# A decoder step on one Trainium2 core: the dense part of the expert lookup narrowed from 384 to 368 tokens, the gathered part widened from 136 to 152

## The chip, the cores and the metric

The kernel is one program on one core of a Trainium2 chip. The metric is its device time in microseconds (us). Three runs of the kernel before took 1760.16, 1762.86 and 1763.15 us, so the median is 1762.86 us. One further execution was profiled and is the source of every row below.

## The reference: what is computed

One decoder layer for 512 prompt tokens and 8 single-token samples (520 tokens, width 1024). A mixer stage (retention and a short convolution) comes first. Then comes the expert lookup, which is the part that matters here:

```
q = xb @ w_q                               # per token: 8 heads x 2 halves x 128
s = q . keys                               # 8 x 2 x 128 scores
s1, i1 = top_k(s[:, :, 0], 16);  s2, i2 = top_k(s[:, :, 1], 16)
cand = s1[..., :, None] + s2[..., None, :]             # 16 x 16 per head
top_s, top_pos = top_k(cand, 16)                       # 16 experts per head
eidx = i1*128 + i2 (at top_pos);  gate = softmax(top_s)    # 128 experts per token, out of 16384
a    = gelu(einsum('pd,ped->pe', xb, u_tab[eidx]))
out  = einsum('pe,ped->pd', gate * a, v_tab[eidx])
```

The result goes through an RMS norm and is added to the residual.

## The kernel before

Every engine has its own program, written out by hand. The queues run in order and meet at semaphores. There is no scheduler.

**First expert stage (up to 1204 us).** For every key row `m` of 128 (128 experts each) TensorE computes the product of all 520 tokens with `u_tab` (L1711: each weight is split in a high and a low part, 3 products x 8 x 2 halves of 260 columns = 48 matmuls). ScalarE applies gelu (L1783), and SyncE stores the 128 x 520 result in DRAM (`ahead_dram`, `keep`). Beside it VectorE picks the experts, tile of tokens by tile of tokens (`select`, `decide`). The tiles are given by `EDGES`. For the first `SCATTERED` = 3 tiles (`ND` = 384 tokens) GpSimd scatters the gates into a dense array in DRAM (`gates_dram`, L99, 384 indirect DMAs with one gate per token each). This array was cleared by 24 DMAs and is laid out in chunks of `CH` = 32 tokens.

**Second expert stage (1204 to 1742 us).** The 128 steps `n` of this stage run over the key rows again, now with `v_tab`. Two ways of summing exist side by side:

- *Dense tokens (the first ND).* SyncE loads the stored products (`aa`, drawn from the buffer `qp`) and the gates (`gt`) for 4 steps at a time (L1615, L1617, two buffers each) and `v_tab` in pairs of 1024 KB (L1595, four buffers). VectorE multiplies products by gates (`coefficients`, L1934). ScalarE rounds to the high part `ch` (L1805) and the weights to `uh` (L1769). VectorE subtracts for the low parts `ul` (`low`, L1905) and `cl` (`low_coefficients`, L1939). TensorE does 3 x 8 = 24 matmuls of ND columns per step (L1734). Only the first 8 matmuls with `cl` at step 0 have 512 columns, to set all columns of the accumulators.
- *Gathered tokens (the other TG = 520 - ND = 136).* The 128 choices of each token are packed so that row `r` of `TG` rows holds one expert for each of 128 partitions. `GROUPS` lists them as (first token, tokens): the 8 samples, then 64 and 64 prompt tokens. With n tokens in a group, each token takes 128/n partitions and the group has n rows. For each row GpSimd issues one indirect DMA for the product (`ag`, L1863, 128 x 4 bytes, issued 8 rows ahead) and one for the expert's `v_tab` row (`vg`, L1870, 128 x 4 KB = 512 KB, four buffers, drawn from `qp`). VectorE adds it, scaled, to the group's sum `fg` (L1955) and first scales `ag` once in 8 rows (L1949). `summed(n)` spreads the rows evenly over the steps n = 8 to 123. After a group's last row TensorE adds its partitions up into the columns of its tokens (`gathered_sums`, L1695, 8 matmuls), at step 72 for the first group of 64 and at step 126 for the second. The group of samples is folded by DMAs and VectorE instead (L1962).

Within one step VectorE's order is: coefficients of step n+2, `ul` of step n, `cl` of step n+1, then the gathered rows that are due. GpSimd may not issue `vg` of row r before VectorE has summed row r-4.

**End (1742 to 1762 us).** Squares, norm and residual over 512 columns. This part does not depend on ND.

Of the kernel before, what the change touches and what calls it, by code (L numbers as in the profile page):

```python
# [9 lines left out]
ALU = mybir.AluOpType  # L10
# [3 lines left out]
P = 128  # L14
# [19 lines left out]
EDGES = (0, 128, 256, 384, 512, T)  # L34
# [4 lines left out]
GROUPS = ((128, 8), (0, 64), (64, 64))  # L39
CH = TT // 4  # L40
# [56 lines left out]
def scatter(nc, io, i, r):  # L97

    nc.gpsimd.indirect_dma_start(  # L99
        out=io["gates"].rearrange("g p c a t -> (g p c a t)").unsqueeze(1),  # L100
        out_offset=bass.IndirectOffsetOnAxis(ap=io["where"][:, i, r:r + 1], axis=0),
        in_=io["gate"][:, i, r:r + 1], in_offset=None, compute_op=ALU.add).then_inc(io["scattered"][i], 16)
# [250 lines left out]
def mixer_stage(nc, sem, sb, pair, halves, residual, on_chip, hh, hl, qp, io, w_dram):  # L353
# [3 lines left out]
    with stack:  # L357
# [178 lines left out]
        def sync_program(sp):  # L536
# [20 lines left out]
            for n in range(NSLOT, len(order)):  # L557
# [4 lines left out]
                if 0 <= c < CLEARS:  # L562
                    size = NGRP * 2 * SCATTERED // CLEARS
                    i, g = divmod(c * size, NGRP)
                    wide = TT // CH // 2
                    sp.dma_start(io["gates"][g:g + size, :, i * wide:(i + 1) * wide]
                                 .rearrange("g p c a t -> p g (c a t)"),
                                 blank[:].unsqueeze(1).to_broadcast([P, size, TT * GB // 2]))\
                        .then_inc(io["cleared"][i // 2], 16)
# [890 lines left out]
def peer_stage(nc, sem, sb, pair, halves, residual, on_chip, hh, hl, packed, qp, io):  # L1460
# [17 lines left out]
    TURN_AT = 72  # L1478
# [18 lines left out]
    with stack:  # L1497
# [26 lines left out]
        fg = sb(stack, "fg", [P, len(GROUPS), D])  # L1524
        folded = keys[:].rearrange("p j n -> p (j n)")[0:P // 2, 0:D]
        packed_choice = sb(stack, "packed_choice", [P, 3, TG])
        chosen = sb(stack, "chosen", [P, GROUPS[1][1]])
        ag = sb(stack, "ag", [P, TG])
# [4 lines left out]
        sample_rows, sample_squares = fg[0:NS, 0, :], folded[0:NS]  # L1533
# [47 lines left out]
        def sync_program(sp):  # L1581
# [54 lines left out]
            def fold(n):  # L1636

                if n:
                    sp.wait_ge(fold_ok, n)
                else:  # L1640
                    sp.wait_ge(fg_ok, GROUP_AT[1])
                w = FOLDS[n]
                sp.dma_start(folded[0:w], fg[w:2 * w, 0, :]).then_inc(fold_in, 16)
# [32 lines left out]
        def tensor_program(pe):  # L1676
# [12 lines left out]
            def gathered_sums(g):  # L1689

                first, n = GROUPS[g]
                pe.wait_ge(fg_ok, GROUP_AT[g + 1])
                pe.wait_ge(chosen_ok, 1)
                for k in range(KD):
                    nc.tensor.matmul(ps[:, k, ND + first:ND + first + n], fg[:, g, k * P:(k + 1) * P],  # L1695
                                     chosen[:], start=False, stop=False)
# [28 lines left out]
            for n in range(NK):  # L1725
# [14 lines left out]
                if n == TURN_AT:  # L1740
                    gathered_sums(1)
                if n == NK - 2:
                    gathered_sums(2)
# [136 lines left out]
        def vector_program(dve):  # L1880
# [61 lines left out]
            def gathered():  # L1942
# [11 lines left out]
                sums_of = fg[:, group_of(r), :]  # L1954
                nc.vector.scalar_tensor_tensor(sums_of, vg[:, r % NG, :], ag[:, r:r + 1], sums_of,  # L1955
                                               ALU.mult, ALU.add).then_inc(fg_ok, 1)

            def fold(n):

                w = FOLDS[n]  # L1960
                dve.wait_ge(fold_in, 16 * (n + 1))
                nc.vector.tensor_tensor(fg[0:w, 0, :], fg[0:w, 0, :], folded[0:w], ALU.add).then_inc(fold_ok, 1)  # L1962
# [23 lines left out]
            for m in range(lows[0], LAST):  # L1986
# [3 lines left out]
                if n == 0:  # L1990
                    coefficients(0)
                    coefficients(1)
                    nc.vector.tensor_scalar(cl[:, 0, ND:SEQ], ident[:, 0:SEQ - ND], 0.0, None, ALU.mult)
                    low_coefficients(0)
                if 0 < n <= len(GROUPS):
                    nc.vector.memset(fg[:, n - 1], 0.0)
                if n == len(GROUPS) + 1:
                    nc.vector.tensor_reduce(chosen[:], ident.rearrange("p (h t) -> p t h", t=GROUPS[1][1]), AX.X,
                                            ALU.add).then_inc(chosen_ok, 1)
# [138 lines left out]
```

## Time and profile before

| | |
|---|---|
| median of three runs | 1762.86 us (1760.16 to 1763.15) |
| the profiled execution | 1764.12 us, its span 1762.3 us |
| mean granted TensorE clock | 0.993 of full speed |
| PE busy | 1729.2 us, 98% of the span |
| DVE, POOL, ACT busy | 62%, 59%, 33% |
| memory traffic | 385.18 MB by DMA, mean 219 GB/s |

PE is TensorE's matmuls, PEld its weight loads, DVE VectorE, ACT ScalarE, POOL GpSimd and SP SyncE. The span runs from the first to the last instruction. Matmuls are pipelined: a single one takes longer from start to end than the distance to the next. So their pace is read from a stretch's length divided by the number of matmuls in it, and not from the mean of one. "share" of DMA is the mean busy share of the core's 16 DMA engines. It can come out slightly above 1, since packets of one engine may overlap.

### The profile page before, as it was taken

How to read it: one execution, taken by the hardware profiler on the slowest of the kernel's cores; microseconds unless marked ns; L12 is line 12 of the kernel's file. 1: busy time of each engine (PE TensorE's matmuls, PEld its weight loads, DVE VectorE, ACT ScalarE, POOL GpSimd, SP SyncE). 2: the span in 40 equal slices, each digit the busy share in tenths (PEclk: the TensorE clock that was granted, in tenths of full speed). 3: DMA queues.
4: the chain of work that ended last, by engine and by line, in shares of the span. 5: the costliest groups of instructions: out<-in, count | busy, mean ns of one | idle time of the engine just before them, and what ended most of it. 6: DMA issues, size and time to landing. Idle time of an engine off the chain costs nothing.

```text
span 1762.3 us, 31194 instructions
## 1 busy us (share of the span) xinstructions
PE 1729.2 (98%) x12708; PEld 1688.9 (96%) x12708; DVE 1097.6 (62%) x2208; ACT 587.3 (33%) x764; POOL 1043.2 (59%) x693
## 2 busy tenths in 40 slices
PE   7999999999999999999999999999999999999996
PEld 5999979699999999999999999999999999999996
DVE  6724686568577366667552221224888989888884
ACT  5222264333323333232232222223333333333332
POOL 0340100006777888888888888874677777767721
PEclk9999999999999999999999999999999999999997
DMA  8523399673566665766667666668999999999971
GB/s 328 195 97 144 99 374 311 224 233 82 109 128 145 127 145 110 151 127 140 143 132 153 138 134 145 133 139 332 360 368 377 378 346 369 368 368 372 377 293 49
DMA packets 192358, 385.18 MB, mean 219 GB/s; under 512 B 74376, under 2 KB 132104, under 8 KB 177368
## 3 DMA queue, kind: packets, MB, share of 16 engines
q1 hardware_dynamic: 111864, 306.56, 51.3%
q0 software_dynamic: 80352, 76.65, 20.2%
q8 instruction: 100, 1.64, 0.4%
q14 instruction: 42, 0.34, 0.1%
HBM read 318.44 MB, written 64.19 MB: 217 GB/s over the span
## 4 chain that ended last, share of the span: by engine, by line
PE 94%; DVE 5%; ACT 1%; issue 0%; DMA 0%; SPq 0%; DVEq 0%; ACTq 0%
PE ps L1711 42%; PE ps L1734 30%; PE ps L669 12%; PE ps L720 3%; PE ps L783 2%; PE ps L615 1%; PE ps L1685 1%; DVE wl L1153 1%; DVE rs L1182 1%; PE ps L807 1%; DVE tg L1372 0%; PE ps L750 0%; DVE first_low L1153 0%; PE ps L736 0%; DVE qp L2022 0%
## 5 line engine op out<-in xcount | busy, mean ns | idle before, releaser
L99 POOL DMA_INDIRECT gates_dram<-gate,where x384 | 643.0, 1675 | 266.3 <-issue 252.2
L1711 PE MATMUL ps<-hh,ul 128*128 128x260 f32 x2048 | 412.8, 283 | 0.0
L1711 PE MATMUL ps<-hl,uh 128*128 128x260 f32 x2048 | 412.8, 283 | 0.0
L1711 PE MATMUL ps<-hh,uh 128*128 128x260 f32 x2048 | 412.1, 283 | 0.0
L1905 DVE TENSOR_TENSOR ul<-us,uh 128x1024 fp32r<-128x1024 f32 x132 | 161.2, 1222 | 350.9 <-issue 291.3
L1734 PE MATMUL ps<-cl,uh 128*128 128x384 f32 (+1 forms) x1024 | 345.0, 337 | 1.6 <-issue 1.1
L1734 PE MATMUL ps<-ch,uh 128*128 128x384 f32 x1024 | 344.1, 336 | 0.0
L1734 PE MATMUL ps<-ch,ul 128*128 128x384 f32 x1024 | 344.1, 336 | 0.0
L1711 PEld LDWEIGHTS ps<-hl,uh 128*128 128x128 f32 x2048 | 315.7, 189 | 0.4 <-issue 0.4
L1711 PEld LDWEIGHTS ps<-hh,ul 128*128 128x128 f32 x2048 | 315.8, 188 | 0.0
L1711 PEld LDWEIGHTS ps<-hh,uh 128*128 128x128 f32 x2048 | 314.8, 188 | 0.0
L1783 ACT ACTIVATE a<-ps 128x520 f32<-128x520 f32 x128 | 77.5, 606 | 520.0 <-PE ps L1711 434.7
L1870 POOL DMA_INDIRECT qp<-vtab,packed_choice x136 | 184.2, 1355 | 102.7 <-DVE fg L1955 74.3
L1863 POOL DMA_INDIRECT ag<-ahead_dram,packed_choice x136 | 167.5, 1232 | 62.1 <-issue 41.2
L1734 PEld LDWEIGHTS ps<-cl,uh 128*128 128x128 f32 x1024 | 192.5, 188 | 2.3 <-issue 1.3
L1734 PEld LDWEIGHTS ps<-ch,ul 128*128 128x128 f32 x1024 | 192.5, 188 | 0.3
L1734 PEld LDWEIGHTS ps<-ch,uh 128*128 128x128 f32 x1024 | 192.5, 188 | 0.0
L1955 DVE SCALAR_TENSOR_TENSOR fg<-qp,ag,fg 128x1024 f32<-128x1024 f32 x136 | 174.1, 1280 | 11.7 <-DMA qp<-vtab,packed_choice 5.9
L1805 ACT ACTIVATE ch<-qp 128x384 fp32r<-128x384 f32 x128 | 67.2, 526 | 337.1 <-PE ps L1734 280.9
L1905 DVE TENSOR_TENSOR ul<-pairs,uh 128x1024 fp32r<-128x1024 f32 x124 | 150.9, 1217 | 0.8 <-ACT uh L1769 0.8
L1153 DVE TENSOR_TENSOR wl<-wr,wh 128x2048 fp32r<-128x2048 f32 x38 | 89.7, 2361 | 81.9 <-ACT wh L911 81.7
L1769 ACT ACTIVATE uh<-us 128x1024 fp32r<-128x1024 f32 x132 | 138.6, 1051 | 0.0
(248 smaller groups left out, 2238.8 us busy)
## 6 DMA issues: line engine op xcount, KB each, us to landing
us<-utab SPq DMA_DIRECT2D x128, 512.0 KB
pairs<-vtab SPq DMA_DIRECT2D x62, 1024.0 KB
gates_dram<-blank SPq DMA_DIRECT2D x24, 1024.0 KB, 10.1
ahead_dram<-a SPq DMA_DIRECT2D x128, 192.0 KB
qp<-ahead_dram SPq DMA_DIRECT2D x32, 768.0 KB
gt<-gates_dram SPq DMA_DIRECT2D x32, 768.0 KB
wr<-w_ada SPq DMA_DIRECT2D x21, 1024.0 KB, 7.9
wr<-w_in SPq DMA_DIRECT2D x13, 1024.0 KB, 4.7
```

The costliest lines, as they stand in the source:

```text
L99: nc.gpsimd.indirect_dma_start(out=io["gates"].rearrange("g p c a t -> (g p c a t)").unsqueeze(1), out_offset=bass.IndirectOffsetOnAxis(ap ...
L669: last = nc.tensor.matmul(pair(m % RING)[:, a, :], w, r[:, k, a * TH:(a + 1) * TH], start=(first and q == 0), stop=(final and q == 2))
L1153: nc.vector.tensor_tensor(low_buffers[b], raw_buffers[raw_slot(split[i])], high_buffers[b].bitcast(F32), ALU.subtract).then_inc(wl_ok, 1)
L1711: last = nc.tensor.matmul(out[:, half, :], w, r[:, k, half * TH:(half + 1) * TH], start=(k == 0 and q == 0), stop=(k == KD - 1 and q == 2))
L1734: last = nc.tensor.matmul(ps[:, k, columns], w, r[:, n % NL, columns], start=whole, stop=(n == NK - 1 and q == 2))
L1769: nc.scalar.activation(uh[:, m % NH], raw(m), ACT.Copy).then_inc(uh_ok, 1)
L1783: nc.scalar.activation(halves(a[:, m % NA]), pair(1 + m % 3), ACT.Gelu_apprx_tanh).then_inc(a_ok, 1)
L1805: nc.scalar.activation(ch[:, n % NL], aa[:, n // GB % NV, n % GB], ACT.Copy).then_inc(ch_ok, 1)
L1863: nc.gpsimd.indirect_dma_start(out=ag[:, at:at + 1], out_offset=None, in_=words, in_offset=bass.IndirectOffsetOnAxis(ap=packed_choice[:, 0 ...
L1870: nc.gpsimd.indirect_dma_start(out=vg[:, r % NG, :], out_offset=None, in_=values, in_offset=bass.IndirectOffsetOnAxis(ap=packed_choice[:, ...
L1905: nc.vector.tensor_tensor(ul[:, m % NH], raw(m), uh[:, m % NH].bitcast(F32), ALU.subtract)\
L1955: nc.vector.scalar_tensor_tensor(sums_of, vg[:, r % NG, :], ag[:, r:r + 1], sums_of, ALU.mult, ALU.add).then_inc(fg_ok, 1)
```

## The change

`EDGES` becomes (0, 128, 256, 368, 496, 520). The third scattered tile has 112 tokens, the two last tiles 128 and 24. ND becomes 368, and TG 152. A fourth group of 16 tokens (8 partitions per token, 16 rows) is summed behind the others. `CH` becomes 16, since 368 is no multiple of 32. The second turn on TensorE moves from step 126 to step 118, and a third one comes at step 126. The fourth sum lies on the `keys` buffer, which is free by then.

```diff
-EDGES = (0, 128, 256, 384, 512, T)
+EDGES = (0, 128, 256, 368, 496, T)
-GROUPS = ((128, 8), (0, 64), (64, 64))
-CH = TT // 4
+GROUPS = ((144, 8), (0, 64), (64, 64), (128, 16))
+CH = 16
@@ scatter
+    n = EDGES[i + 1] - EDGES[i]
-        out_offset=bass.IndirectOffsetOnAxis(ap=io["where"][:, i, r:r + 1], axis=0),
-        in_=io["gate"][:, i, r:r + 1], in_offset=None, compute_op=ALU.add).then_inc(io["scattered"][i], 16)
+        out_offset=bass.IndirectOffsetOnAxis(ap=io["where"][0:n, i, r:r + 1], axis=0),
+        in_=io["gate"][0:n, i, r:r + 1], in_offset=None, compute_op=ALU.add).then_inc(io["scattered"][i], 16)
@@ peer_stage
-    TURN_AT = 72
+    TURNS_AT = (72, 118, NK - 2)
-        fg = sb(stack, "fg", [P, len(GROUPS), D])
+        fg = sb(stack, "fg", [P, len(GROUPS) - 1, D])
+        on_keys = keys[:].rearrange("p j n -> p (j n)")
+        chosen_last = sb(stack, "chosen_last", [P, GROUPS[3][1]])
+        sums_of = [fg[:, g, :] for g in range(len(GROUPS) - 1)] + [on_keys[:, D:2 * D]]
@@ gathered_sums
-                pe.wait_ge(chosen_ok, 1)
+                pe.wait_ge(chosen_ok, 2)
-                    nc.tensor.matmul(ps[:, k, ND + first:ND + first + n], fg[:, g, k * P:(k + 1) * P],
-                                     chosen[:], start=False, stop=False)
+                    nc.tensor.matmul(ps[:, k, ND + first:ND + first + n], sums_of[g][:, k * P:(k + 1) * P],
+                                     (chosen if n == GROUPS[1][1] else chosen_last)[:], start=False, stop=False)
@@ tensor_program, behind step n
-                if n == TURN_AT:
-                    gathered_sums(1)
-                if n == NK - 2:
-                    gathered_sums(2)
+                if n in TURNS_AT:
+                    gathered_sums(1 + TURNS_AT.index(n))
@@ vector_program, behind step n
                 if 0 < n <= len(GROUPS):
-                    nc.vector.memset(fg[:, n - 1], 0.0)
+                    nc.vector.memset(sums_of[n - 1], 0.0)
                 if n == len(GROUPS) + 1:
                     nc.vector.tensor_reduce(chosen[:], ident.rearrange("p (h t) -> p t h", t=GROUPS[1][1]), AX.X,
                                             ALU.add).then_inc(chosen_ok, 1)
+                    nc.vector.tensor_reduce(chosen_last[:], ident.rearrange("p (h t) -> p t h", t=GROUPS[3][1]), AX.X,
+                                            ALU.add).then_inc(chosen_ok, 1)
```

The rest of the diff adapts the 24 clearing DMAs to 23 chunks and the zeros of `cl` to 144 columns. Since `pack` loops over the groups, it issues 12 small DMAs and not 9. Since the loop over chunks in the mixer's last part runs to TT/CH, 4 more tiny VectorE operations compute `token`.

**VectorE, from the gathered row of step 10 to that of step 11** of the second expert stage (`fg` is the sum of gathered rows, `qp` the products, `ul` and `cl` the low parts). Before:

```order
L1955 SCALAR_TENSOR_TENSOR fg<-qp,ag,fg 128x1024
L1934 TENSOR_TENSOR qp<-qp,gt 128x384
L1905 TENSOR_TENSOR ul<-pairs,uh 128x1024
L1939 TENSOR_TENSOR cl<-qp,ch 128x384
L1955 SCALAR_TENSOR_TENSOR fg<-qp,ag,fg 128x1024
```

The same place now:

```order
L1958 SCALAR_TENSOR_TENSOR fg<-qp,ag,fg 128x1024
L1937 TENSOR_TENSOR qp<-qp,gt 128x368
L1908 TENSOR_TENSOR ul<-pairs,uh 128x1024
L1942 TENSOR_TENSOR cl<-qp,ch 128x368
L1958 SCALAR_TENSOR_TENSOR fg<-qp,ag,fg 128x1024 x2
```

The chain of a step is the same, with 368 instead of 384 elements in two of its operations. A step with two gathered rows comes at 8, 11, 14 and 17, where before it came at 8, 13 and 19: 152 rows instead of 136 stand in the same 116 steps.

**TensorE, at step 126.** `chosen` and `chosen_last` are the 0/1 matrices that add up a token's partitions. Before:

```order
L1734 MATMUL ps<-ch,uh 128x384
L1734 MATMUL ps<-ch,ul 128x384
L1695 MATMUL ps<-chosen,fg 128x64 x8
L1734 MATMUL ps<-cl,uh 128x384
L1734 MATMUL ps<-ch,uh 128x384
```

Now:

```order
L1739 MATMUL ps<-ch,uh 128x368
L1739 MATMUL ps<-ch,ul 128x368
L1700 MATMUL ps<-chosen_last,keys 128x16 x8
L1739 MATMUL ps<-cl,uh 128x368
L1739 MATMUL ps<-ch,uh 128x368
```

The 8 matmuls with 64 columns that stood here stand 8 steps earlier, at step 118, and 8 with 16 columns are new. On GpSimd the alternation of `ag` and `vg` is the same, and 16 pairs longer.

## Rows read from the trace of the kernel before

**Rows 1.** The page: PE's total; 40 slices of DMA share and GB/s.

```profile
PE 1729.2 (98%) x12708; PEld 1688.9 (96%) x12708; DVE 1097.6 (62%) x2208; ACT 587.3 (33%) x764; POOL 1043.2 (59%) x693
...
DMA  8523399673566665766667666668999999999971
GB/s 328 195 97 144 99 374 311 224 233 82 109 128 145 127 145 110 151 127 140 143 132 153 138 134 145 133 139 332 360 368 377 378 346 369 368 368 372 377 293 49
```

**Rows 2.** Chain that ended last: start, length in us, what, how many instructions.

```profile
811.15 392.32 PE ps L1711 x3264
...
1204.61 238.35 PE ps L1734 x1368
...
1511.57 224.69 PE ps L1734 x1296
1736.27 1.73 PE ps L1695 x16
```

**Rows 3.** Line L1734: duration min/median/max in ns, first and last start.

```profile
L1734 PE MATMUL ps<-ch,ul x1024: 332/336/339, 1205.1 to 1741.9; 128*128 128x384 f32 x171
```

**Rows 4.** Steady stretch on DVE: start, us, operation; "x2" is two merged.

```profile
1479.89 2.67 DVE L1955 SCALAR_TENSOR_TENSOR fg<-qp,ag,fg 128x1024 f32<-128x1024 f32 x2
1482.47 0.55 DVE L1934 TENSOR_TENSOR qp<-qp,gt 128x384 f32<-128x384 f32 x1
1482.94 1.22 DVE L1905 TENSOR_TENSOR ul<-pairs,uh 128x1024 fp32r<-128x1024 f32 x1
1484.08 0.55 DVE L1939 TENSOR_TENSOR cl<-qp,ch 128x384 fp32r<-128x384 f32 x1
1484.55 1.28 DVE L1955 SCALAR_TENSOR_TENSOR fg<-qp,ag,fg 128x1024 f32<-128x1024 f32 x1
1485.74 0.55 DVE L1934 TENSOR_TENSOR qp<-qp,gt 128x384 f32<-128x384 f32 x1
```

**Rows 5.** Windows: length, busy us of each engine, PEclk, DMA share, GB/s.

```profile
1240.00:1700.00 460.00, 459.57 (x2656) 459.00 (x2656) 401.87 (x486) 163.75 (x223) 327.83 (x253) 1.00 0.98 369
...
1205.00:1710.00 505.00, 504.57 (x2914) 503.72 (x2913) 434.72 (x530) 179.97 (x244) 351.73 (x272) 1.00 0.97 366
```

**Rows 6.** DMA queues from 1240 to 1700 us: MB and share of 16 engines.

```profile
q1 hardware_dynamic: 16020, 101.48, 57.1%
q0 software_dynamic: 22512, 67.71, 40.2%
```

**Rows 7.** Windows with the densest DMA: mixer's weight loads; within the second stage.

```profile
230.00:270.00 40.00, 39.32 (x269) 32.02 (x269) 34.81 (x31) 23.95 (x36) 0.55 (x1) 1.00 1.04 393
...
1302.00:1332.00 30.00, 30.00 (x175) 30.00 (x174) 25.84 (x32) 10.92 (x15) 20.31 (x17) 1.00 1.02 377
```

**Rows 8.** The page, costliest groups on POOL: count, busy, mean ns, idle before.

```profile
L1870 POOL DMA_INDIRECT qp<-vtab,packed_choice x136 | 184.2, 1355 | 102.7 <-DVE fg L1955 74.3
L1863 POOL DMA_INDIRECT ag<-ahead_dram,packed_choice x136 | 167.5, 1232 | 62.1 <-issue 41.2
```

**Rows 9.** POOL in order of time: first wait for DVE; the last gather.

```profile
1238.00 1.95 POOL L1870 DMA_INDIRECT qp<-vtab,packed_choice  x1 [5.61 <-DVE fg L1955]
1240.26 1.31 POOL L1863 DMA_INDIRECT ag<-ahead_dram,packed_choice  x1 [0.30 <-issue]
...
1702.00 1.01 POOL L1870 DMA_INDIRECT qp<-vtab,packed_choice  x1 [1.12 <-DVE fg L1955]
```

**Rows 10.** Waits on DVE from 1210 to 1740 us: total, times, longest.

```profile
DVE cl L1939 <- ACT ch L1805: 45.1, 57, 2.5
...
DVE fg L1955 <- DMA qp<-vtab,packed_choice: 5.9, 5, 2.4
```

**Rows 11.** Line L1955: first and last start of the 136 gathered sums.

```profile
L1955 DVE SCALAR_TENSOR_TENSOR fg<-qp,ag,fg x136: 1267/1279/1312, 1236.4 to 1716.6; 128x1024 f32<-128x1024 f32 x136
```

More of the change, by code:

```diff
@@ L565, in sync_program @@
                     wide = TT // CH // 2
-                    sp.dma_start(io["gates"][g:g + size, :, i * wide:(i + 1) * wide]
-                                 .rearrange("g p c a t -> p g (c a t)"),
-                                 blank[:].unsqueeze(1).to_broadcast([P, size, TT * GB // 2]))\
+                    last = min((i + 1) * wide, NCH)
+                    some = (last - i * wide) * GB * CH
+                    sp.dma_start(io["gates"][g:g + size, :, i * wide:last].rearrange("g p c a t -> p g (c a t)"),
+                                 blank[:, 0:some].unsqueeze(1).to_broadcast([P, size, some]))\
                         .then_inc(io["cleared"][i // 2], 16)
@@ L1523, in peer_stage @@
         cl = sb(stack, "cl", [P, NL, SEQ], F32R)
[L1524 to L1525 removed]
+        fg = sb(stack, "fg", [P, len(GROUPS) - 1, D])
+        on_keys = keys[:].rearrange("p j n -> p (j n)")
+        folded = on_keys[0:P // 2, 0:D]
         packed_choice = sb(stack, "packed_choice", [P, 3, TG])
         chosen = sb(stack, "chosen", [P, GROUPS[1][1]])
+        chosen_last = sb(stack, "chosen_last", [P, GROUPS[3][1]])
         ag = sb(stack, "ag", [P, TG])
@@ L1532, in peer_stage @@
         squares = qp[:, 0:KD, :]
-        sample_rows, sample_squares = fg[0:NS, 0, :], folded[0:NS]
+        sums_of = [fg[:, g, :] for g in range(len(GROUPS) - 1)] + [on_keys[:, D:2 * D]]
+        sample_rows, sample_squares = sums_of[0][0:NS], folded[0:NS]
         ON_POOL = (0, 2, 4)
@@ L1642, in fold @@
                 w = FOLDS[n]
-                sp.dma_start(folded[0:w], fg[w:2 * w, 0, :]).then_inc(fold_in, 16)
+                sp.dma_start(folded[0:w], sums_of[0][w:2 * w]).then_inc(fold_in, 16)
             for m in range(NW, NK + 2 * FIRST_PAIR):
@@ L1953, in gathered @@
                     dve.wait_ge(fg_ok, r)
-                sums_of = fg[:, group_of(r), :]
-                nc.vector.scalar_tensor_tensor(sums_of, vg[:, r % NG, :], ag[:, r:r + 1], sums_of,
+                total = sums_of[group_of(r)]
+                nc.vector.scalar_tensor_tensor(total, vg[:, r % NG, :], ag[:, r:r + 1], total,
                                                ALU.mult, ALU.add).then_inc(fg_ok, 1)
@@ L1961, in fold @@
                 dve.wait_ge(fold_in, 16 * (n + 1))
-                nc.vector.tensor_tensor(fg[0:w, 0, :], fg[0:w, 0, :], folded[0:w], ALU.add).then_inc(fold_ok, 1)
+                nc.vector.tensor_tensor(sums_of[0][0:w], sums_of[0][0:w], folded[0:w], ALU.add).then_inc(fold_ok, 1)
             def sample_sums():
@@ L1992, in vector_program @@
                     coefficients(1)
-                    nc.vector.tensor_scalar(cl[:, 0, ND:SEQ], ident[:, 0:SEQ - ND], 0.0, None, ALU.mult)
+                    nc.vector.tensor_scalar(cl[:, 0, ND:SEQ], cst[:, 0:2].rearrange("p a n -> p (a n)")[:, 0:SEQ - ND],
+                                            0.0, None, ALU.mult)
                     low_coefficients(0)
                 if 0 < n <= len(GROUPS):
-                    nc.vector.memset(fg[:, n - 1], 0.0)
+                    nc.vector.memset(sums_of[n - 1], 0.0)
                 if n == len(GROUPS) + 1:
                     nc.vector.tensor_reduce(chosen[:], ident.rearrange("p (h t) -> p t h", t=GROUPS[1][1]), AX.X,
+                                            ALU.add).then_inc(chosen_ok, 1)
+                    nc.vector.tensor_reduce(chosen_last[:], ident.rearrange("p (h t) -> p t h", t=GROUPS[3][1]), AX.X,
                                             ALU.add).then_inc(chosen_ok, 1)
```

## The prediction, made before the changed kernel ran

> **What bounds the kernel now.** I read the page first. TensorE is busy for 98% of the span, and from 1204 us on the DMA digits stand at 9 with 346 to 378 GB/s, where the stage before has 6 [rows 1]. Then the chain: it stays on TensorE, with 392 us of line L1711 and 238 + 225 us of L1734, so this engine sets the time in both expert stages [rows 2]. The second stage begins at 1204.6 us and its last matmul starts at 1741.9 and takes 0.3, so it ends at 1742.2 [rows 2, 3].
>
> The third view is the windows. From 1240 to 1700 us TensorE has no gap worth a microsecond (459.6 of 460), but the 16 DMA engines are 98% busy [rows 5]. That makes two nearly full resources side by side, and the change relieves one and loads the other. The reader should look for the slack of each feeder: VectorE waits 45 us for `ch`, which is a wait for TensorE's pace, and only 6 us for gathered rows [rows 10], and GpSimd waits 74 us for VectorE to free a buffer [rows 8].
>
> **TensorE, the gain.** At 384 columns the pace is 224.69/1296 = 173.4 ns per matmul, at 260 columns 392.32/3264 = 120.2 ns [rows 2]. That is 53.2 ns for 124 columns, 0.429 ns a column, and 6.9 ns for 16. All but the 8 whole ones of the 128 x 24 = 3072 matmuls lose 16 columns: 3064 x 6.9 = 21.0 us. A step then takes 24 x 166.5 = 4.00 us instead of 4.16. A weight load or another fixed cost is no floor here, since the 120 ns of the narrower matmul lie far below 166. The third turn adds 8 matmuls. The one with 64 columns takes 1.73 us [rows 2]. With 16 columns it should be no more, and not below nothing; I take 1.7, the only row of its kind. The turn moved from step 126 to 118 costs the same at either place. TensorE alone gives 21.0 - 1.7 = 19.3 us.
>
> **VectorE, hidden.** In a stretch without waits, a step with one gathered row takes 1485.74 - 1482.47 = 3.27 us, and two rows take 1482.47 - 1479.89 = 2.58 where one takes 1.19, so a second row adds 1.39 [rows 4]. The two operations of 384 elements take 0.47 us apart, so 16 elements less save about 0.02 each. With 152/116 = 1.31 rows per step this comes to 3.23 + 0.31 x 1.39 = 3.66 us, and 0.02 for scaling `ag`: 3.7 against TensorE's 4.00. The inner runs of 16 gates instead of 32 are unknown. The operation on runs of 32 lies within 0.01 us of the one on whole rows [rows 4], so I take nothing. Below nothing is excluded, as the elements are the same; the upper end is the pitch doubled, 0.47 more, which would make VectorE the bound at 4.15. One more memset and one more reduction fall into steps 4 and 5, before gathered rows start. VectorE's order puts the row's sum in front of the next step's `ul` and `cl`, so what delays a row delays TensorE two operations later.
>
> **DMA, where the gain goes.** Taken away are 16 tokens of `aa` and `gt`: 64 loads x 16 x 4 x 4 bytes x 128 partitions = 2.1 MB. Added are 16 gathers of 512 KB: 8.4 MB. From 1240 to 1700 us the gathers' queue moved 67.71 MB in 40.2% of 460 us, 2.73 us per MB of all 16 engines' time, and SyncE's queue 101.48 MB in 57.1%, 2.59 us per MB [rows 6]. So the change adds 8.4 x 2.73 - 2.1 x 2.59 = 22.9 - 5.4 = 17.5 us. The window from 1205 us to the end of the traffic at 1710 had 505 x 0.97 = 490 us of such work [rows 5], so now it has 507.5. With all engines always busy that ends at 1712.5, 2.5 us later than before, while TensorE would like to be 19 us earlier.
>
> What is left after the last landing: the row's sum, a product and `ul`, 1.28 + 0.47 + 1.2 = 3.0 us [rows 4], then steps 124 to 127 with 4 x 4.00 and the turn with 1.7 [rows 2], 20.7 in all. Before, it was 1742.2 - 1710 = 32.2: the last sum started only at 1716.6 [rows 11], and VectorE ran ahead of TensorE. These 11.5 us of slack are eaten first. The stage then ends at 1712.5 + 20.7 = 1733.2 instead of 1742.2, 9.0 us earlier.
>
> **GpSimd, the same answer by another way.** A pair of `ag` and `vg` takes 1.232 + 1.355 us and twice 0.30 of issue, 3.19 us [rows 8, 9]. TensorE's pace asks for a row each 4.00 / 1.31 = 3.05 us. So GpSimd, which had time to wait before (one row per 3.55 us), falls behind by 0.13 us per row. At 1238.0 it starts `vg` of row 4, the first that has to wait for VectorE [rows 9]. Row 143, the last with an `ag` beside it, starts 139 x 3.19 = 443 us later, at 1681, and has landed 5 to 8 us on; 8 is the bound from the last gather at 1702.0 and the end of the traffic at 1710 [rows 5, 9]. It is due at step 117. Behind it stand 3.0 us of VectorE and steps 118 to 127 with two turns, 40.0 + 3.5. The stage ends between 1732.5 and 1735.5: 7 to 10 us earlier.
>
> **Other edits, at nothing.** The scattering of 112 tokens instead of 128 is on GpSimd beside TensorE's unbroken first stage, and the second stage's start hardly hangs on it: the first stage's chain ends at 811.15 + 392.32 = 1203.47 and the next starts at 1204.61 [rows 2], so no wait above 1.1 us stands there. At worst an indirect DMA of 112 costs what one of 128 does. The 3 small DMAs of `pack` and the 4 operations for `token` fall in stages where the DMA digit is mostly 6 [rows 1] and VectorE's work lies beside TensorE's.
>
> **The sum.** Profiled execution 1764.1 us, less 9.0 by the DMA way and 7 to 10 by GpSimd's: 1755.1. The median of the runs is 1.3 us below the profiled one, which gives 1753.8. The two limits work together (a late gather stalls VectorE, which frees the buffers later), so I add one: 1755 us.
>
> **Rivals.**
>
> *The full gain.* The DMA engines can do more than they did. In the mixer they ran at a share of 1.04 for 40 us with 393 GB/s, and for 30 us of this stage at 1.02 [rows 7]. At 1.03 throughout, the traffic ends at 1205 + 507.5/1.03 = 1698 and would allow a stage end of 1718, so TensorE's 1742.2 - 19.3 = 1722.9 decides, and GpSimd would have to give 0.1 us per pair. Against it: 1.02 came with only 377 GB/s. Median 1743.6. Chance 24%.
>
> *Slower: the traffic keeps its rate.* If the 2 to 3% of idle share are structural (transfers come in bursts, behind buffers that VectorE frees), the window grows with the work: 507.5/0.97 = 523, end 1728.2, stage end 1748.9, 6.7 us later than before, median 1769.6. By bytes, (366 x 505 = 184.8, + 6.3) MB at 369 GB/s take 517.9 us, stage end 1743.6, median 1764.3. It decides from 507.5/516.5, a share of 0.983, downward: almost exactly what the stage has now [rows 5]. Against it: so far TensorE set the pace, so nothing asked for more. Chance 17%.
>
> The Trainium skill has a rule that speaks for this one (DMA: Bandwidth & Descriptors, Specifications): the memory side limits a core to about 358 GB/s, and the vendor's cost model uses 368. The trace agrees as far as it goes, with 366 to 369 in this stage [rows 5], but its 393 in the mixer are above it [rows 7]. By 368 as a ceiling the estimate is 191.1 MB in 519.3 us, a stage end at 1745.0 and a median of 1765.7.
>
> *No difference* within what a measurement of this kernel can tell (0.2%, 3.5 us): slack and loss cancel, with GpSimd's pair at 3.25 us. Median 1763. Chance 15%. That the narrower matmul is not faster I hold for excluded by the two paces.
>
> **How the numbers follow.** The partly eaten gain has 44%, with its own range 1748 to 1760; nearly all of it is beyond 0.2%. Faster 0.67 (24 and 43), same 0.16, slower 0.17. The range for 8 in 10 is 1743 to 1768: it takes in the full gain, and of the slower case most.
>
> **What would show it.** In the changed profile L1739 should have a pace of 166 to 167 ns where TensorE runs unbroken; a different number makes the first step wrong. From about step 60 on TensorE should show waits for `ul` or `cl`, 8 to 12 us in all, and the chain there should pass through VectorE's gathered sums. VectorE's wait for `vg` should grow from 6 to 20 us or more, GpSimd's 74 us of waiting for VectorE should fall below 30, and the DMA share should be 0.99 to 1.01 with 375 to 390 GB/s. If the share stays at 0.97 while TensorE waits, the slower rival holds; if TensorE does not wait, the full gain does. A VectorE product longer than 0.6 us would make my cost of the shorter runs wrong.

## The result, and the profile after

The changed kernel takes 1780.22 us (median of 4 runs, 1777.43 to 1784.77), the kernel before 1762.67 us in the same job. The ratio is 1.0100, with a 95% interval of 1.0076 to 1.0124. It is slower by some 17 us, where 8 us faster was forecast, and it lies outside the range of 1743 to 1768.

The profiled execution took 1777.43 us with a span of 1775.6. It is the fastest of the four and 13 us slower than the profiled one of before, so what the traces show accounts for 13 us of the 17. First the page, against [rows 1]:

```profile
PE 1721.2 (97%) x12724; PEld 1675.5 (94%) x12724; DVE 1112.5 (63%) x2232; ACT 585.6 (33%) x764; POOL 1095.5 (62%) x725
...
DMA  8424298663566675756667666678999999999971
GB/s 349 170 96 166 89 392 295 239 210 65 103 126 144 120 150 117 154 109 150 129 141 160 135 141 142 133 199 325 371 378 379 375 348 350 364 362 381 384 308 49
...
PE 67%; POOL 18%; DVE 6%; issue 5%; DMA 3%; ACT 1%; DVEq 0%; SPq 0%; ACTq 0%
```

TensorE is busy for 8 us less, as its work has become less, yet the span is 13 us longer. The DMA digits and GB/s of the second stage are nearly those of before. The last line, the chain by engine, is what is new: 18% of the span now goes over POOL. The same line before:

```profile
PE 94%; DVE 5%; ACT 1%; issue 0%; DMA 0%; SPq 0%; DVEq 0%; ACTq 0%
```

A piece of the new chain (start, length, what):

```profile
1461.45 1.28 POOL ag L1866
1463.04 1.97 POOL qp L1873
1465.31 4.06 POOL ag L1866
1469.67 7.62 DMA qp<-vtab,packed_choice
1477.33 1.28 DVE fg L1958
...
1708.72 4.29 PE ps L1739 x24
1713.01 1.73 PE ps L1700 x16
1714.74 32.22 PE ps L1739 x192
1746.96 1.69 PE ps L1700 x16
```

GpSimd issues `ag` and `vg` in turn without a pause, the row has landed 7.62 us after its issue began, and VectorE, which has been waiting, sums it. Where TensorE runs unbroken it takes 32.22/192 = 167.8 ns per matmul. The turn with 16 columns (1.69 us) costs what one with 64 does (1.73); the 8 matmuls of a turn stand as 16 instructions in the trace. The stage starts and ends as follows, against 1204.6 to 1742.2 before [rows 2, 3]:

```profile
L1739 PE MATMUL ps<-cl,uh x1024: 327/328/675, 1201.9 to 1752.1; 128*128 128x368 f32 x169, 128*128 128x512 f32 x2
...
L1739 PE MATMUL ps<-ch,ul x1024: 325/328/508, 1202.4 to 1752.4; 128*128 128x368 f32 x171
```

With the last 0.4 us it ends at 1752.8: 550.9 us instead of 537.6. The waits in it, from 1202 to 1752 us (total, times, longest), stand for [rows 10] and for the 74.3 of [rows 8]:

```profile
PE ps L1739 <- DVE ul L1908: 10.8, 11, 2.3
PE ps L1739 <- issue: 8.6, 6, 2.9
...
DVE fg L1958 <- DMA qp<-vtab,packed_choice: 37.8, 34, 2.8
DVE cl L1942 <- ACT ch L1808: 18.1, 14, 4.8
...
POOL qp L1873 <- DVE keys L1958: 11.9, 7, 2.6
POOL qp L1873 <- DVE fg L1958: 9.8, 10, 3.1
```

TensorE, which waited for 1.5 us before, now waits for 19.4. VectorE waits for rows for 38 us instead of 6, and GpSimd for VectorE only 21.7 instead of 74.3: it has become the engine that is behind. The windows have the columns of [rows 5]:

```profile
1240.00:1690.00 450.00, 432.19 (x2524) 425.27 (x2523) 390.46 (x474) 154.07 (x211) 360.44 (x273) 0.99 0.98 369
1205.00:1710.00 505.00, 486.06 (x2842) 478.39 (x2841) 434.74 (x532) 174.07 (x238) 395.42 (x301) 0.99 0.98 369
```

PEclk fell below 1.00, which it did not before. A timeline of TensorE and two windows show where:

```profile
1274.80 0.33 PE L1739 MATMUL ps<-ch,ul 128*128 128x368 f32 x1
1277.41 0.68 PE L1739 MATMUL ps<-cl,uh 128*128 128x368 f32 x1 [2.28 <-DVE ul L1908]
1277.88 0.51 PE L1739 MATMUL ps<-ch,uh 128*128 128x368 f32 x1
1278.19 0.51 PE L1739 MATMUL ps<-ch,ul 128*128 128x368 f32 x1
```

```profile
1277.40:1284.30 6.90, 6.89 (x32) 6.89 (x33) 6.73 (x9) 1.27 (x3) 4.74 (x5) 0.75 0.94 331
...
1482.80:1490.00 7.20, 7.18 (x26) 7.18 (x27) 7.10 (x9) 0.32 (x1) 5.01 (x4) 0.57 0.88 285
```

After 2.28 us of waiting, matmuls start every 0.31 us instead of every 0.167: the lower of the two clock levels. This comes twice, after two of the three waits above 2 us, with 10 and 19 matmuls at 0.31 us: 4 us on top of the waits themselves.

The stage's balance from the distances between starts: 537.6 before, less 3072 x 5.7 ns = 17.6 (173.3 became 167.6), plus 1.7 for the turn, 22.1 more in pauses (the listed waits and what the engine needs to start again), 4.0 at the low clock and 3.1 in single slow matmuls, most of them the first after a pause, gives 550.9. The stage also began 2.7 us earlier than before, which is within what its start varies by over the profiled kernels here (1201.9 to 1206.8 us).

After the stage, 22.8 us follow instead of 20.1. The work there has not grown: VectorE's last operation ends 16.2 us behind the stage, against 16.1. What has grown is the last wait of the program, SyncE for the end of TensorE's queue, before and now (total, times, longest):

```profile
SPq L325 <- PEq L325: 1.6, 1, 1.6
```

```profile
SPq L326 <- PEq L326: 4.2, 1, 4.2
```

In all runs below it goes with the number of `ag` and `vg` issues: 0.2 us in the four without `ag`, 1.6 with 136 of each, 2.9 with 144, 4.2 with 152. Nothing of the prediction speaks of it, and why it is so is open.

### The profile page after: what moved, and what is told of

It is laid out like the page before. It is cut to its first block, busy times and chain, and to the rows that moved or that the text cites. A ratio compares the mean times of both kernels' runs of the same rounds, so it can differ in the third digit from the quotient of the medians.

```text
span 1775.6 us, 31302 instructions
## 1 busy us (share of the span) xinstructions
PE 1721.2 (97%) x12724; PEld 1675.5 (94%) x12724; DVE 1112.5 (63%) x2232; ACT 585.6 (33%) x764; POOL 1095.5 (62%) x725
## 4 chain that ended last, share of the span: by engine, by line
PE 67%; POOL 18%; DVE 6%; issue 5%; DMA 3%; ACT 1%; DVEq 0%; SPq 0%; ACTq 0%
PE ps L1716 42%; PE ps L671 12%; POOL qp L1873 9%; POOL ag L1866 8%; PE ps L1739 3%; DMA qp<-vtab,packed_choice 3%; PE ps L722 3%; PE ps L785 2%; PE ps L617 1%; PE ps L1690 1%; DVE fg L1958 1%; DVE wl L1155 1%; DVE rs L1184 1%; DVE ul L1908 1%; PE ps L809 0%
## 5 line engine op out<-in xcount | busy, mean ns | idle before, releaser
L1739 PE MATMUL ps<-cl,uh 128*128 128x368 f32 (+1 forms) x1024 | 342.4, 334 | 19.7 <-DVE ul L1908 10.8
L1739 PE MATMUL ps<-ch,uh 128*128 128x368 f32 x1024 | 339.7, 332 | 0.0
L1739 PE MATMUL ps<-ch,ul 128*128 128x368 f32 x1024 | 339.6, 332 | 0.0
L1873 POOL DMA_INDIRECT qp<-vtab,packed_choice x152 | 211.4, 1391 | 65.4 <-issue 43.7
L1866 POOL DMA_INDIRECT ag<-ahead_dram,packed_choice x152 | 191.4, 1259 | 66.7 <-issue 46.0
L1958 DVE SCALAR_TENSOR_TENSOR fg<-qp,ag,fg 128x1024 f32<-128x1024 f32 x136 | 174.2, 1281 | 52.4 <-DMA qp<-vtab,packed_choice 37.8
L1808 ACT ACTIVATE ch<-qp 128x368 fp32r<-128x368 f32 x128 | 65.5, 512 | 352.6 <-PE ps L1739 285.3
## 6 DMA issues: line engine op xcount, KB each, us to landing
gates_dram<-blank SPq DMA_DIRECT2D x20, 1024.0 KB, 10.5
```

Source lines behind the costliest of these rows:

```text
L1739: last = nc.tensor.matmul(ps[:, k, columns], w, r[:, n % NL, columns], start=whole, stop=(n == NK - 1 and q == 2))
L1808: nc.scalar.activation(ch[:, n % NL], aa[:, n // GB % NV, n % GB], ACT.Copy).then_inc(ch_ok, 1)
L1866: nc.gpsimd.indirect_dma_start(out=ag[:, at:at + 1], out_offset=None, in_=words, in_offset=bass.IndirectOffsetOnAxis(ap=packed_choice[:, 0 ...
L1873: nc.gpsimd.indirect_dma_start(out=vg[:, r % NG, :], out_offset=None, in_=values, in_offset=bass.IndirectOffsetOnAxis(ap=packed_choice[:, ...
L1958: nc.vector.scalar_tensor_tensor(total, vg[:, r % NG, :], ag[:, r:r + 1], total, ALU.mult, ALU.add).then_inc(fg_ok, 1)
```

## The experiments

Each run is compared with the kernel before on the same chip (medians 1763.05 to 1763.83 us from run 1 on). Theory G: GpSimd can't issue the gathers as fast as the narrower step asks. Theory D: the DMA engines are full. Theory R: four row buffers are too few.

**Run 1: no `ag` DMAs.**

```diff
-                    nc.gpsimd.indirect_dma_start(
-                        out=ag[:, at:at + 1], out_offset=None, in_=words, ...).then_inc(ag_in[at // GCH % 4], 16)
+                    pass
```

> The changed kernel without its 152 indirect DMAs for the products of gathered tokens (ag is a constant instead; that part of the computation is left out). Everything else stays: 152 gathers of 512 KB, VectorE's sums, TensorE's work. The DMA traffic falls by 152 x 512 bytes only. Theory G (GpSimd issues a row in 3.25 us where TensorE's pace asks for 3.05): a row now costs about 1.4 + 0.3 = 1.7 us, GpSimd waits for VectorE again, TensorE has no waits in the second stage, its clock no dips, and the time is about 1744 us (the 19 us of narrower matmuls below 1763). Theory D (the 16 DMA engines are the bound): the traffic is the same, so the time stays at 1775 to 1785 us. Theory R (four buffers are too few for a gather's latency): it stays above 1770 us, too, since the latency of vg does not change.

Measured: 1755.04 us, ratio 0.9952 [0.9936, 0.9969], so 25 us less than the changed kernel (4 of them in the program's last wait). GpSimd's row on the page:

```profile
L1870 POOL DMA_INDIRECT qp<-vtab,packed_choice x152 | 223.6, 1471 | 295.2 <-DVE fg L1954 242.6
```

GpSimd now waits for VectorE for 243 us, so its rate is no limit, and the loss is more than made good. But 11 us of TensorE's gain are missing: with four buffers a row is asked for only when its buffer comes free, 10 to 11 us ahead of its sum, and an issue that takes 8.1 us (at 1372 and at 1419 us) then shows in full. G was right in sign and too bold by 11 us; D fell.

**Run 2: gathers of half the bytes.**

```diff
-                        out=vg[:, r % NG, :], out_offset=None, in_=values,
+                        out=vg[:, r % NG, 0:D // parts], out_offset=None,
+                        in_=io["vtab"].rearrange("a b (x d) -> (a b x) d", x=parts),
```

> The changed kernel in which each gather from the fifth on fetches 2 KB per partition instead of 4 KB (half of each row is stale and the rows are others: that part of the computation is left out). The number of GpSimd instructions and VectorE's work stay, the traffic falls by 148 x 256 KB = 39 MB, a fifth of the second stage's. Theory D: time about 1744 us. Theory G: GpSimd's pair still takes about 3.25 us, so the time stays within 6 us of the changed kernel's 1780, and DMA share falls to about 0.88. Theory R: a shorter landing helps in part, 1755 to 1770 us.

Measured: 1768.18 us, 1.0029 [1.0010, 1.0048]. The window from 1240 to 1690 us:

```profile
1240.00:1690.00 450.00, 437.67 (x2574) 432.58 (x2573) 398.25 (x484) 157.16 (x215) 362.80 (x278) 0.99 0.83 296
```

The DMA share falls from 0.98 to 0.83, and still TensorE waits for 12 us, VectorE for 40 us for rows, and an `ag` and a `vg` take 1.299 + 1.328 us. With a sixth of the engines' time free, full DMA engines aren't what holds the rows. But G's own forecast, within 6 us of 1780, is missed, and the time lies in theory R's range. The 12 us won over the changed kernel fit shorter landings (a row's sum starts 7.8 us after its issue, in the median, instead of 9.6). So how long a row takes to land counts beside the rate.

**Run 3: five row buffers.**

```diff
-    NH, NA, NV, NL, NG = 3, 2, 2, 3, 4
+    NH, NA, NV, NL, NG = 3, 2, 2, 3, 5
```

> The changed kernel with five buffers for gathered rows instead of four. Theory R: GpSimd's waits for VectorE (22 us) vanish, late rows are bridged, time 1750 to 1760 us. Theory G: GpSimd's own 3.25 us per row stays; only the 22 us of waits for a buffer can shrink, so 1765 to 1780 us. Theory D: no change, 1775 to 1785 us.

Measured: 1767.48 us, 1.0025 [1.0001, 1.0049]. That is 13 us better, in G's range and not in R's, and still not faster than before. GpSimd waits for VectorE for only 13 us, rows come 3.28 us apart. Depth covers the long issues, not the rate.

**Run 4: the kernel before with chunks of 16 tokens.**

```diff
-CH = TT // 4
+CH = 16
```

> The kernel before with only the gates' chunks changed from 32 to 16 tokens (384 dense and 136 gathered tokens as before). Theory C (the shorter runs cost VectorE or the scattering something): above 1766 us, with VectorE's product longer than 0.55 us. Theories G, D and R: the chunks are innocent, 1760 to 1766 us.

Measured: 1763.38 us, 1.0000 [0.9987, 1.0013]. The product of gates takes 553 ns as before (551). The shorter runs are innocent.

**Run 5: no `ag` DMAs and five buffers** (runs 1 and 3 together).

> The changed kernel without the DMAs for ag (constant instead, left out) and with five buffers for gathered rows. Without ag but with four buffers the time was 1755 us, not the 1744 that TensorE's pace gives. Theory R' (what was left there is the ring: a row's sum starts 10.7 us after its gather, so four buffers give a row per 3.0 us at best): the fifth buffer gives 1744 to 1748 us. Theory D' (what was left is DMA bandwidth, 383 GB/s at a share of 0.98): it stays at 1752 to 1758 us.

Measured: 1746.40 us, 0.9880 [0.9834, 0.9927]. The window, and GpSimd's waits for VectorE (total, times, longest):

```profile
1240.00:1690.00 450.00, 450.00 (x2697) 449.77 (x2696) 419.88 (x509) 164.00 (x225) 214.29 (x146) 1.00 1.00 394
```

```profile
POOL qp L1870 <- DVE fg L1954: 221.5, 100, 21.0
```

This settles D: with all 16 tokens' rows to fetch, 394 GB/s flow for 450 us, TensorE never stops, and almost the full gain is there. What held the changed kernel is the issue of `ag` together with the ring's depth: either cure alone leaves it at 1755 or 1767 us. One doubt is left here, since without `ag` its small packets are missing too; run 8 keeps them.

**Run 6: five buffers, rows spread over two more steps at each end.**

```diff
-    NH, NA, NV, NL, NG = 3, 2, 2, 3, 4
-    G0 = 8
+    NH, NA, NV, NL, NG = 3, 2, 2, 3, 5
+    G0 = 6
```

> The changed kernel with five buffers and the gathered rows spread over steps 6 to 125 instead of 8 to 123, complete computation. Theory G: GpSimd needs 152 x 3.25 = 494 us from 1205 us on whatever the schedule, so it pays that it starts to wait less: the last row lands at 1707 instead of about 1717, and 120 steps instead of 116 ask for a row per 3.16 us, not 3.05; time 1750 to 1760 us. Theory D: the traffic decides and does not change, 1765 to 1780 us as with five buffers alone (1767).

Measured: 1767.81 us, 1.0010 [0.9987, 1.0033], the same as run 3. The expectation of G was missed, and the time lies in D's range, though runs 5 and 8 exclude what D says. One `ag` took 10.5 us, and `ag` + `vg` with their gaps took 3.24 us, where the spread asks for 120 x 4.02/152 = 3.17.

```profile
1421.90 10.54 POOL L1866 DMA_INDIRECT ag<-ahead_dram,packed_choice  x1 [0.30 <-issue]
```

**Run 7: 144 gathered tokens, 376 dense, chunks of 8, four buffers.**

```diff
-EDGES = (0, 128, 256, 368, 496, T)
-GROUPS = ((144, 8), (0, 64), (64, 64), (128, 16))
-CH = 16
+EDGES = (0, 128, 256, 376, 504, T)
+GROUPS = ((136, 8), (0, 64), (64, 64), (128, 8))
+CH = 8
```

> Half the step: 376 dense and 144 gathered tokens, chunks of 8 tokens, a last group of 8 tokens; four buffers, complete computation. TensorE alone would give 3064 x 8 x 0.43 ns = 10.5 us less 1.7 for the third turn, 1754 us. A row is asked for every 4.08 / 1.24 = 3.29 us, just above GpSimd's 3.25. Theory G with a sharp knee: 1754 to 1758 us. If slips near the knee count already (long GpSimd instructions of 4 to 8 us that nothing makes up for): 1760 to 1768 us. Theory D: traffic grows by half of before, 1763 to 1772 us.

Measured: 1781.27 us, 1.0092 [1.0062, 1.0122], no better than 152 tokens and a clear miss. TensorE still waits for 13.9 us for `ul` (issues of 11.0, 8.9 and 6.9 us), though a row is asked for only each 116 x 4.14/144 = 3.33 us: the pair, at 1.312 + 1.458 and two gaps, took 3.37. And the narrower matmul gains next to nothing by itself, which led to runs 12 to 14.

**Run 8: sums over 128 of 1024 columns** (the issue and the bytes stay; VectorE's two-input operation becomes short).

```diff
-                nc.vector.scalar_tensor_tensor(total, vg[:, r % NG, :], ag[:, r:r + 1], total,
+                nc.vector.scalar_tensor_tensor(total[:, 0:P], vg[:, r % NG, 0:P], ag[:, r:r + 1], total[:, 0:P],
```

> The changed kernel in which VectorE's sum of a gathered row covers 128 instead of 1024 columns (the rest is left out). GpSimd's instructions and all DMA traffic stay. Theory L (GpSimd's instructions last 1.3 us instead of 0.95 because they wait for a running VectorE instruction): with VectorE idle half of the time a pair of ag and vg falls from 3.25 to about 2.7 us and the time to about 1744 us, unless DMA binds. Theory G without L: the pair stays at 3.25 us and the time above 1765. Theory D: the time stays above 1770 us, with GpSimd waiting for free buffers.

Measured: 1757.22 us, 0.9948 [0.9923, 0.9973].

```profile
L1866 POOL DMA_INDIRECT ag<-ahead_dram,packed_choice x152 | 187.8, 1235 | 68.5 <-issue 46.0 <-DMA ahead_dram<-a 22.4
L1873 POOL DMA_INDIRECT qp<-vtab,packed_choice x152 | 179.1, 1179 | 74.3 <-issue 33.9 <-DVE fg L1958 25.9 <-DVE keys L1958 14.5
```

The pair with its gaps falls from 3.25 to 3.01 us, just under the 3.05 asked for, and TensorE's waits from 19 to 3 us. So GpSimd's issue is slowed by VectorE's work, less than I had expected (2.7); the other two-input operations stayed. All 304 issues and all bytes are there, and the window from 1240 to 1690 us shows what the DMA engines can do with them:

```profile
1240.00:1690.00 450.00, 446.83 (x2659) 445.28 (x2658) 283.81 (x502) 162.08 (x223) 339.02 (x282) 1.00 1.01 390
```

390 GB/s with `ag` in place close the doubt left by run 5. That VectorE slows the issue shows in the changed kernel, too: its 14 issues beside which VectorE did nothing at all took 0.94 to 0.95 us, the 290 others 1.29 in the median. One place: VectorE stands still from 1270.88 to 1274.47, and GpSimd's operations inside that time are short.

```profile
1274.47 1.29 DVE L1958 SCALAR_TENSOR_TENSOR fg<-qp,ag,fg 128x1024 f32<-128x1024 f32 x1 [3.59 <-issue]
```

```profile
1270.18 1.52 POOL L1873 DMA_INDIRECT qp<-vtab,packed_choice  x1 [0.30 <-issue]
1272.01 0.95 POOL L1866 DMA_INDIRECT ag<-ahead_dram,packed_choice  x1 [0.31 <-issue]
1273.26 0.95 POOL L1873 DMA_INDIRECT qp<-vtab,packed_choice  x1 [0.30 <-issue]
```

The Trainium skill (SBUF — State Buffer, SBUF: two separate sides) says that VectorE and GpSimd share one port pair, which whoever starts first holds for the whole instruction; an operation of VectorE with two SBUF inputs counts only against a GpSimd operation that reads SBUF. The 0.95 against 1.28 us would agree if the issue of an indirect DMA is such an operation, which no run here shows. That the port is the cause isn't shown either, only that VectorE's work is.

**Run 9: the kernel before with five buffers** (the edit of run 3).

> The kernel before (136 gathered tokens) with five row buffers instead of four, nothing else. Theory G (GpSimd's rate of issuing the gathers sets the second stage once there are more than some 140 rows; at 136 rows GpSimd has 74 us to spare and TensorE waits for almost nothing): no difference, 1760 to 1764 us, TensorE's waits in the stage below 2 us as before. Rival R (the ring's depth is what costs time in every version, since it took 13 us off at 152 rows): 1750 to 1757 us.

Measured: 1762.66 us, 0.9989 [0.9975, 1.0004]. No difference, as G says.

**Run 10: the kernel before without the `ag` DMAs** (the edit of run 1).

> The kernel before without the DMAs that fetch one gate value per row (ag); the sums take a constant in their place, so this part of the computation is left out. Theory G: 136 rows are within GpSimd's reach with or without these issues, so the time stays within 2 us of the kernel before, 1760 to 1764 us; the 25 us that the same cut took off at 152 rows are a cost of 152 rows alone. Rival C (these issues cost time in every version, through the queues or through VectorE's port): 1750 us or less.

Measured: 1760.17 us, 0.9984 [0.9967, 1.0000]. The cut that took off 25 us at 152 rows takes off 3 here, at the edge of what can be told. The stage itself is 536.8 us instead of 537.6. All kernels without `ag` run 18.0 to 18.7 us after the stage instead of 20.1, which is most of the rest, and 1.4 of it is the program's last wait. So of the distance to the kernel before in runs 1, 5 and 14 some 2 us are not the second stage's.

**Run 11: as run 7, with five buffers and the wider spread of run 6.**

> A complete kernel with 144 gathered and 376 dense tokens, chunks of 8, five row buffers, rows spread over steps 6 to 125 instead of 8 to 123. It asks for one row per 3.26 us, GpSimd needs about 3.25 to 3.37. Theory G: near the rate's balance, and TensorE's step is 1.5 us per 8 columns shorter in 128 steps (10.5 us in all) less what GpSimd's long operations cost: 1755 to 1762 us. Rival S (chunks of 8 or the short third tile make GpSimd's gathers longer, as the four-buffer version of it with 3.37 us per pair hinted): the pair stays at 3.35 us or more, and the time at 1768 us or more.

Measured: 1767.81 us, 1.0017 [1.0000, 1.0034]. `ag` + `vg` took 1.316 + 1.348 with 0.6 of gaps, 3.26 us, where 120 x 4.14/144 = 3.45 are asked for (the 3.26 of the expectation was miscounted, and so is the 3.19 of run 13's: 120 x 4.09/144 = 3.41). The time misses G's range and all but reaches rival S's, whose pair of 3.35 us isn't there. GpSimd has 49 us to spare, and what TensorE still waits for, 4.5 us once at 1506, stands behind an issue of 10.1 us at 1492. For another 4 us it stood still ahead of the stage, as in the profiles of runs 7, 9 and 13; why is open. But my 10.5 us of narrower matmuls weren't there. The chain, with four numbers to divide:

```profile
1518.81 190.27 PE ps L1739 x1104
1709.08 1.73 PE ps L1700 x16
1710.81 33.14 PE ps L1739 x192
```

190.27/1104 = 172.3 ns at 376 columns, against 173.3 at 384. One by one, the distances between starts form a pattern of three steps (at 376 one of the three has 175 and 176 most of the time), and the operand `ch` lies in three slots, 376 or 368 words apart. In the kernel before the slots are 384 words apart, and every distance is 173 or 174.

**Runs 12 to 14: slots of `ch` 384 words apart**, with the columns read unchanged; in run 3's kernel, run 11's and run 5's.

```diff
-        ch = sb(stack, "ch", [P, NL, ND], F32R)
+        ch = sb(stack, "ch", [P, NL, 3 * P], F32R)
...
-                nc.scalar.activation(ch[:, n % NL], aa[:, n // GB % NV, n % GB], ACT.Copy).then_inc(ch_ok, 1)
+                nc.scalar.activation(ch[:, n % NL, 0:ND], aa[:, n // GB % NV, n % GB], ACT.Copy).then_inc(ch_ok, 1)
```

> The 152-token kernel with five row buffers (1767.5 us), and the slots of ch in SBUF set 384 words apart instead of 368; the same columns are read. Theory A (the matmul pitch of 167.6 ns instead of 166.7 comes from where the moving operand's slots begin: its pattern repeats with the three slots, and slots of 384 words show 173.33 ns without any pattern): pitch flat at 166.7 ns, 2.9 us less of matmuls, time 1764 to 1767 us. Rival W (it is the width, which is no multiple of something the engine wants): pitch 167.6 with its pattern, time unchanged.

> The complete 144-token kernel with five row buffers (1767.8 us), slots of ch 384 words apart instead of 376. Theory A: pitch 170.0 ns instead of 172.3, 7 us less of matmuls, median 1758 to 1763 us. But the gathers are asked for in 3.19 us per row instead of 3.23, so GpSimd may take back some of it: up to 1766. Rival W: pitch still 172.3 ns and 1767 us or more.

> As the 152-token kernel with five row buffers and without the DMAs for ag (1746.4 us; its output lacks that part), with slots of ch 384 words apart. There TensorE waits for nothing, so the pitch shows in full in the time: by theory A 166.7 ns, 2.9 us less, median 1743 to 1744 us; by rival W 1746 us.

Measured: run 12 1771.21 us, 1.0062 [1.0042, 1.0082]; run 13 1761.01 us, 0.9991 [0.9973, 1.0009]; run 14 1743.56 us, 0.9894 [0.9878, 0.9911]. The longest unbroken piece of the chain in run 5, 13 and 14, in this order:

```profile
1501.83 185.10 PE ps L1739 x1104
```

```profile
1509.95 188.26 PE ps L1739 x1104
```

```profile
1499.87 182.50 PE ps L1739 x1095
```

At 368 columns the pace goes from 167.7 to 166.7 ns, at 376 from 172.3 to 170.5, and the three steps are alike. So theory A holds and rival W falls. One thing is not separated: `cl`, the other moving operand, is declared behind `ch`, and may begin elsewhere now. Where nothing else waits the time follows: run 14 is 2.8 us below run 5, and run 13 is 7 us below run 11. In run 12 the median does not: with 1771.2 us (1765.7 to 1777.3) it is no better than run 3's, and its expectation was missed. Its profiled execution, the fastest of its five, has the shorter stage (538.6 us against 543.9 in run 3's), with 10 us of waits on GpSimd and 12.7 on TensorE. That GpSimd can't follow the quicker step fits this, but no trace shows the slower executions. Run 13 is the best complete kernel, and can't be told from the kernel before.

## Why the prediction was wrong, by its own steps

**TensorE, the gain: right in kind, mis-sized.** I took 0.429 ns a column and 6.9 ns per matmul from two widths. Measured is 5.7 ns (173.3 to 167.6), 17.5 us instead of 21.0. Of the missing 3.5 us 2.9 are the slots of `ch`, which came with the change and which I never looked at; runs 5 and 14 show them. With them put right the term is (173.3 - 166.7) x 3064 = 20.2 us, 18.5 net where I had 19.3, and run 14's stage is 518.7 us, 18.9 less than before. The price of the third turn, 1.7 us, was right.

**VectorE, hidden: right.** The product takes 0.53 to 0.54 us with shorter runs, and run 4 shows no cost. VectorE is late only behind rows.

**DMA, where the gain goes: refuted.** The slack of 11.5 us and the end of the traffic at 1712.5 came from holding 0.97 to 1.00 of share to be the limit. In run 5 the share is 1.00 with 394 GB/s for 450 us, 25 GB/s more than before moved in [rows 5], and TensorE doesn't wait. Run 8 has 390 at 1.01 with every issue in place. The share of 0.98 with 369 GB/s was no sign that the engines could do no more. As a ceiling for this core, the 358 and 368 GB/s of the rule that I weighed don't hold either, as [rows 7] hinted. The Trainium skill (HBM Reference, Specifications (TRN2)) has the other rule that I should have set against it: a core that streams alone goes well above its share, to about 425 GB/s. The 394 of run 5 agree, as they are above the share; 425 was not reached.

**GpSimd, the same answer by another way: the step that failed.** It named the right engine and was 17 us short, 16 of them in one term: 3.19 us per row was the time of the issues alone, and the rows came 3.31 us apart. It had row 143's `vg` start at 1681, the row land within 8 us, and the stage end at 1735.5 at the latest. The two rows in question, and GpSimd's two groups against [rows 8]:

```profile
1233.71 1.95 POOL L1873 DMA_INDIRECT qp<-vtab,packed_choice  x1 [3.15 <-DVE fg L1958]
...
1693.35 1.08 POOL L1873 DMA_INDIRECT qp<-vtab,packed_choice  x1 [0.30 <-issue]
```

```profile
L1873 POOL DMA_INDIRECT qp<-vtab,packed_choice x152 | 211.4, 1391 | 65.4 <-issue 43.7
L1866 POOL DMA_INDIRECT ag<-ahead_dram,packed_choice x152 | 191.4, 1259 | 66.7 <-issue 46.0
```

By terms:
- Start: 1233.7 instead of 1238.0, 4.3 us earlier.
- Rate: (1693.35 - 1233.71)/139 = 3.307 us per row instead of 3.19, 16.3 us in all. The pair itself has grown by 0.06 to 3.25, 8.3 us; why is open, as VectorE's busy share beside it is the same (87% in both windows). The rest, 8 us, is mostly waiting for a buffer: the ring makes each late sum a late issue. I had taken the rate as issue alone.
- Landing: row 143's sum starts at 1702.6, 9.2 us after its issue instead of 8.
- Tail: from there to the end of the stage it took 50.2 us, and my 3.0 + 40.0 + 3.5 is 3.7 less. Ten steps and two turns took 44.1. What I left out is row 144, due in the same step 117: its sum starts 3.2 us behind row 143's, and TensorE's next step 6.1 us behind it, not 3.0.

1735.5 - 4.3 + 16.3 + 1.2 + 3.7 = 1752.4, and the stage ended at 1752.8.

**The sum.** "The two limits work together, so I add one" was the second error. GpSimd's lateness, the ring and TensorE's clock feed each other. Each long issue (7.30 us at 1419, 4.06 at 1465) uses up most of what a ring of some 9.6 us holds, and two of the stops, 2.28 and 2.91 us long, were followed by matmuls at half the clock. Not every stop has a long issue behind it. Before the one at 1277 all issues were of usual length, and the row issued at 1263.7 was summed only at 1274.5, 10.8 us later: with no reserve a slow landing is enough. At 136 rows the same issues hit an engine with 74 us to spare: 5.7 us at 1416.9, and TensorE's unbroken line in [rows 5]. That reserve is what the change spent. Besides, 2.6 us of the longer time lie in the program's last wait, a term that the sum has not at all.

**The rivals.** "Slower" came true, for none of the reasons I gave: the traffic did keep its rate (369 GB/s), but as an effect of the late rows, as runs 5 and 8 show. "No difference" had the right mechanism, a pair at 3.25 us, and stopped at the loss of the gain, as if a stage could not go below zero.

**What would show it.** Held: GpSimd's waits below 30 us (21.7), VectorE's above 20 (37.8), and its product below 0.6. Failed: the pace of 166 to 167 ns, by a little (167.6, the slots of `ch`); TensorE's waits of 8 to 12 us (19.4), and from step 60 on (the first is at step 18); and the DMA share of 0.99 to 1.01 with 375 to 390 GB/s (0.98, 369). The chain passes through VectorE's sums, but most of it in this stage is GpSimd's issues, 17% of the span. By my own sign, a share that stays while TensorE waits, the slower rival would now hold. The sign was no good: late issues look the same.

**Open.** What makes single issues last 4 to 11 us: their times and lengths repeat between programs of one kind (7.3 us near 1412 to 1419 in the changed kernel and runs 2, 3 and 12; 8.1 us twice in runs 1, 5 and 14), but what sets them wasn't found. Nor was it found why the program's last wait grows with the issues. Fetching several `ag` columns with one DMA would cut the issues; no run tried it.

## What to carry to other kernels

When work moves from a busy engine to a chain of small issues, divide the issuing engine's whole cycle (operation, gap, and its waits for the ring) by the count, and compare that with the pace that the relieved engine will then have. Then ask how far the answer is from turning over. By my own terms 3.19 us per row meant 7 us won, and 3.24 would have meant nothing won; over 139 rows each 0.05 us is 7 us, and it came to 3.31. A reserve of waiting, here GpSimd's 74 us, absorbs rare long operations, and it fails before it is gone: in run 7 GpSimd still waited 35 us for buffers, and TensorE 14 us behind it. When a width changes, look at where the slots of the operand then begin.

## What the runs showed of the hardware

- A matmul of this stage with a moving operand of 368 columns starts every 166.7 ns with slots 384 words apart and every 167.6 with slots 368 words apart; at 376 columns 170.5 and 172.3. At 384 columns it is 173.3. The edit between the two changes only the slots' distance (and with it, perhaps, where the next buffer begins).
- The 16 DMA engines moved 394 GB/s at a share of 1.00 for 450 us on this core (run 5), and at a share of 0.98 anything from 369 (the changed kernel) to 383 GB/s (run 1). The share alone doesn't tell how much room is left.
- An indirect DMA's issue holds GpSimd for 0.95 us while VectorE is still, mostly 1.28 while it works, and now and then 4 to 11 us (10.5 in run 6, 11.0 in run 7), with 0.30 us between two issues.
- After 2.28 and 2.91 us of waiting TensorE ran at the lower clock level (1.2 of 2.4 GHz) for the next 10 and 19 matmuls (PEclk 0.75 and 0.57 in windows of 7 us), 4 us beside the 19 us of waits; after another wait, of 2.62 us at 1445, it did not.
- 16 matmuls with 16 columns take 1.69 us, with 64 columns 1.73.
- The program's last wait grows with the indirect DMAs issued: 1.6, 2.9 and 4.2 us at 272, 288 and 304 gathers, 0.2 at 136 and 152.
